# Weight halves stored in 16 KB runs, and three waits moved, in a one-layer transformer and mixture-of-experts step

## What is computed

```python
def expert_choice_moe(h, w_router, w_gate, w_up, w_down):
    cap = CAPACITY_FACTOR * T // N_EXPERTS              # 64 latent, 16 context
    logits = einsum('btd,de->bte', h, w_router)
    aff = softmax(logits, axis=-1)
    g, idx = top_k(swapaxes(aff, 1, 2), cap)            # per expert
    xg = h[idx]                                         # gathered rows
    a = einsum('becd,edf->becf', xg, w_gate)            # 1024 x 1024 each
    u = einsum('becd,edf->becf', xg, w_up)
    y = einsum('becf,efd->becd', silu(a) * u, w_down) * g[..., None]
    return zeros.at[idx].add(y)                         # scatter-add
```

## Time and profile before

| | us |
|---|---|
| three runs | 948.62, 950.81, 950.79 |
| median | 950.79 |
| the profiled execution | 950.83 |
| its span, first to last instruction | 948.8 |
| TensorE busy | 887.2 (94% of the span) |
| VectorE, ScalarE, GpSimd busy | 365.1, 216.3, 102.2 |
| mean DMA rate over the span | 284 GB/s |

### The profile page before, as it was taken

One profiled execution on the slowest core, in us unless ns is written; L12 is line 12 of the kernel. 1 busy time (PEld: TensorE's weight loads), 2 busy tenths in 40 slices (PEclk: granted clock), 3 DMA queues, 4 the chain that ended last, 5 costly groups with the idle time before them and its releaser, 6 DMA issues. The chain is left out here.

```text
span 948.8 us, 19908 instructions
## 1 busy us (share of the span) xinstructions
PE 887.2 (94%) x8641; PEld 441.1 (46%) x8641; DVE 365.1 (38%) x974; ACT 216.3 (23%) x528; POOL 102.2 (11%) x137
## 2 busy tenths in 40 slices
PE   3999998899999999889999999999999999999984
PEld 3544444777656565633443443344344343433431
DVE  4255635887767765812031021111113120220135
ACT  3132223766544653410000000000000000000012
POOL 1021200000000000100011011011101101110225
PEclk9999999999899999999999999999999999999997
DMA  9997532300001115979999999999999999999984
GB/s 340 346 368 276 221 135 100 118 1 1 2 1 46 45 46 220 400 270 411 398 398 398 409 398 397 410 398 398 397 409 398 396 409 398 398 408 376 354 303 158
DMA packets 77717, 269.31 MB, mean 284 GB/s; under 512 B 6208, under 2 KB 9984, under 8 KB 77632
## 3 DMA queue, kind: packets, MB, share of 16 engines
q1 hardware_dynamic: 72384, 251.42, 67.7%
q0 software_dynamic: 4160, 13.90, 5.1%
q10 hardware_dynamic: 1088, 2.74, 0.7%
HBM read 252.06 MB, written 15.99 MB: 283 GB/s over the span
## 5 line engine op out<-in xcount | busy, mean ns | idle before, releaser
L954 PE MATMUL ps<-ring,reg 128*32 128x512 f32 x1792 | 201.6, 592 | 0.0
L1814 DVE TENSOR_SCALAR mod<-ps,kt 64x512 f32<-64x512 f32 x30 | 22.5, 749 | 260.6 <-PE ps L954 260.4
L954 PEld LDWEIGHTS ps<-ring,reg 128*32 128x32 f32 x1792 | 58.4, 110 | 113.0 <-issue 104.6
L968 PE MATMUL ps<-ring,values_in 128*32 128x256 f32 x1536 | 92.4, 382 | 4.6 <-DMA ring<-in_w_up 2.3
L1325 ACT ACTIVATE reg<-ps 128x256 f32<-128x256 f32 x16 | 6.2, 385 | 361.8 <-PE ps L1008 361.8
L954 PE MATMUL ps<-ring,kt 128*32 128x512 f32 x768 | 86.8, 592 | 0.0
L810 PE MATMUL ps<-ring,reg 128*128 128x512 f32 x160 | 78.1, 615 | 0.0
L968 PEld LDWEIGHTS ps<-ring,values_in 128*32 128x32 f32 x1536 | 49.3, 110 | 54.8 <-issue 14.6
L656 PE MATMUL ps<-ring,reg_qt 128*128 128x512 f32 x160 | 70.6, 594 | 0.0
L968 PE MATMUL ps<-ring,reg 128*32 128x256 f32 x1024 | 62.9, 388 | 5.6 <-DMA ring<-in_w_down 4.6
L1268 ACT ACTIVATE ring<-ps 128x640 f32<-128x640 f32 (+3 forms) x80 | 44.3, 554 | 74.9 <-PE ps L739 72.4
(11 more groups left out here) (238 smaller groups left out, 999.4 us busy)
## 6 DMA issues: line engine op xcount, KB each, us to landing
ring<-in_w_up SPq DMA_DIRECT2D x32, 2048.0 KB, 23.7
ring<-in_w_down SPq DMA_DIRECT2D x32, 2048.0 KB, 26.2
ring<-in_w_gate SPq DMA_DIRECT2D x16, 2048.0 KB
reg_qt<-in_w_gate SPq DMA_DIRECT2D x16, 2048.0 KB
ring<-in_w_ada SPq DMA_DIRECT2D x12, 2048.0 KB, 14.7
reg<-in_x_sample SPq DMA_DIRECT2D x8, 512.0 KB, 6.2
ring<-in_w_in SPq DMA_DIRECT2D x2, 2048.0 KB, 17.1
ring<-in_w_out SPq DMA_DIRECT2D x2, 2048.0 KB, 10.1
```

What stands on the lines that cost most here:

```text
L954: last = pe.matmul(o[64 * n + r:64 * n + r + 32, :], x(4 * hf + j, r), w[:, j, n * HALF:(n + 1) * HALF], start=(hf == 0 and j == 0), stop= ...
L968: last = pe.matmul(o[32 * q:32 * q + 32, :], x(c), w[:, j, q * QUART:(q + 1) * QUART], start=(c == 0), stop=(c == KC - 1))
L1814: dve.tensor_scalar(put_l[:, n * HALF:(n + 1) * HALF], ps[rows, 3, :], g_l[rows, e:e + 1], None, ALU.mult)
```

## The change

It has two parts.

The first moves waits. Expert 0's gate halves (slots 0 and 1) now wait for the last scores, and only slot 2 and what follows wait for the last product with the values. The wait for the first latent gather ahead of expert 1's gate is gone. On TensorE `turn_lists` goes ahead of `turn_rows_c(1)`, and the filler matmuls between them are dropped. On ScalarE the copy of the turned context activations goes ahead of the second `modulate_c`.

The second gives partition p the rows `4 p + j` (j from 0 to 3) of each half, which lie together in DRAM: a 16 KB run for each partition where there were four of 4 KB. The contraction then needs its other operand in the same order. So every transpose that feeds it takes every fourth column (`feature_block`, and `j:HALF:4` for the latent activations); the modulation's columns are made in four transposes where there were two, with more small copies; the router weights and the pre-FFN gains are loaded in that order, by nine more DMAs. For the context activations the order is made earlier: in the gate and up products `product_c` reads its moving operand with a step of four elements (16 bytes), in two runs of 128 (`by_block`). The down products and all of `product_l` read their weights as before, element by element in a row.

```diff
+        def feature_block(row, c):
+            return row.rearrange("p (h q j) -> p h j q", h=2, j=4)[:, c // 4, c % 4, :]
...
-        N_CONSTS = 10
+        N_CONSTS = 19
...
+                wr_rows = A["w_router"][0].rearrange("(h p j) e -> h p j e", h=2, j=4)
+                sp.dma_start(wr[:, 0:4 * E].rearrange("p (c e) -> p c e", e=E),
+                             wr_rows[0]).then_inc(consts_in, 16)
+                sp.dma_start(wr[:, 4 * E:].rearrange("p (c e) -> p c e", e=E), wr_rows[1]).then_inc(consts_in, 16)
+                ffn_columns = A["g_pre_columns"].rearrange("(q j) (m h b) -> b h m q j", j=4, m=2, h=2)
+                for b, h in itertools.product(range(4), range(2)):
+                    sp.dma_start(gpre[32 * b:32 * b + 32, KC + 4 * h:KC + 4 * h + 4], ffn_columns[b][h][1],
+                                 allow_slow_non_contiguous=True).then_inc(consts_in, 16)
...
             def expert_weight(e, kind, half, s):
                 w = (A["w_gate"], A["w_up"], A["w_down"])[kind]
-                src = w[0].rearrange("e (c p) n -> e p c n", p=P)[e][:, 4 * half:4 * half + 4, :]
-                sp.dma_start(ring_slot(s).rearrange("p (c n) -> p c n", c=4), src).then_inc(slot_in[s], 16)
+                src = w[0].rearrange("e (h p j) n -> e h p (j n)", h=2, j=4)[e][half]
+                sp.dma_start(ring_slot(s), src).then_inc(slot_in[s], 16)
...
             for s in range(SLOTS):
                 sp.wait_ge(*freed[unit_before(len(UNITS), s)])
                 if s == 0:
+                    sp.wait_ge(scores_done, len(HEAD_UNITS))
+                if s == 2:
                     sp.wait_ge(pv_done, len(HEAD_UNITS) // 2)
                 expert_weight(0, s // 2, s % 2, s)
-            sp.wait_ge(scores_done, len(HEAD_UNITS))
             sp.wait_ge(rows_c_stored, 16)
             sp.wait_ge(rows_stored, 16 * LT)
             sp.wait_ge(x1_turned, 2 * TILES)
-            sp.wait_ge(gathered_l, 16)
...
-                for j in range(2):
-                    last = pe.transpose(ps[:, 7, j * P:(j + 1) * P], modq[:, m, j * P:(j + 1) * P], ident[:, :])
+                for j in range(4):
+                    last = pe.transpose(ps[0:P // 2, 7, j * P:(j + 1) * P], modq[:, m, j:QUART:4], ident[:, :])
...
-                    last = pe.transpose(ps[:, 5 + c // 4, c % 4 * P:(c % 4 + 1) * P], xg_l[:, c * P:(c + 1) * P], ident[:, :])
+                    last = pe.transpose(ps[:, 5 + c // 4, c % 4 * P:(c % 4 + 1) * P], feature_block(xg_l, c), ident[:, :])
...
+                by_block = ring_slot(s).rearrange("p (c h q j) -> p c h j q", c=4, h=2, j=4)
...
                     for q in range(4):
                         last = pe.matmul(o[32 * q:32 * q + 32, :], x(c),
-                                         w[:, j, q * QUART:(q + 1) * QUART], start=(c == 0), stop=(c == KC - 1))
+                                         w[:, j, q * QUART:(q + 1) * QUART] if down else by_block[:, j, q // 2, 2 * (q % 2):2 * (q % 2) + 2, :],
+                                         start=(c == 0), stop=(c == KC - 1))
...
-                    last = pe.transpose(TA[:, j * P:(j + 1) * P], a_l[:, j * P:(j + 1) * P], ident[:, :])
+                    last = pe.transpose(TA[:, j * P:(j + 1) * P], a_l[:, j:HALF:4], ident[:, :])
...
             product_c(3, GC[:, QUART:], context_of(0)).then_inc(up_c, 1)
+            turn_lists()
             turn_rows_c(1)
-            keep_busy(3, 4)
-            turn_lists()
...
             silu_c()
+            copy_turned_c(0)
             modulate_c(1)
-            copy_turned_c(0)
...
             def columns(m):
                 n = COLS[m]
                 dve.wait_ge(modcol_done, n + 3)
                 for cond in (0, 1):
+                    for u in (0, 1):
+                        part = slice(P // 2 * u, P // 2 * (u + 1))
+                        last = dve.tensor_copy(cmod[part, n, cond, :].rearrange("p (h j) -> p h j", h=2), cols[:, u, :, :, cond])
+                if n % 2:
+                    dve.wait_ge(consts_in, 16 * N_CONSTS)
+                    link(last)
+                    for cond in (0, 1):
+                        g = gpre[:, (n // 2) * KC:(n // 2 + 1) * KC]
+                        last = dve.scalar_tensor_tensor(cmod[:, n, cond, :], cmod[:, n, cond, :], 1.0, g, ALU.add, ALU.mult)
                 last.then_inc(modcol_ready, 1)
```

More of the change, by code:

```diff
@@ L823, in turn_x1 @@
                     last = pe.transpose(out_at(o)[:, half, c * P:(c + 1) * P],
-                                        xr[:, t, (4 * half + c) * P:(4 * half + c + 1) * P], ident[:, :])
+                                        feature_block(xr[:, t, :], 4 * half + c), ident[:, :])
                 last.then_inc(x1_turned, 1)
@@ L925, in turn_rows_c @@
                 for c in range(KC):
-                    last = pe.transpose(ps[:, 5 + c // 4, c % 4 * P:(c % 4 + 1) * P], xg_c[:, c * P:(c + 1) * P], ident[:, :])
+                    last = pe.transpose(ps[:, 5 + c // 4, c % 4 * P:(c % 4 + 1) * P], feature_block(xg_c, c), ident[:, :])
                 last.then_inc(xc_turned, 1)
@@ L957, in product_l, with product_c @@
                 return last
-            def product_c(s, o, x, arriving=False):
+            def product_c(s, o, x, down=False, arriving=False):
                 w = ring_slot(s).rearrange("p (c n) -> p c n", c=4)
+                by_block = ring_slot(s).rearrange("p (c h q j) -> p c h j q", c=4, h=2, j=4)
                 hf = s % 2
@@ L1024, in expert @@
                 pe.wait_ge(actT_c_ready, e + 1)
-                product_c(4, YC[:, 0:QUART], acts_c)
+                product_c(4, YC[:, 0:QUART], acts_c, down=True)
                 if final:
                     weight_in(5, e)
-                    product_c(5, YC[:, 0:QUART], acts_c).then_inc(down_c, 1)
+                    product_c(5, YC[:, 0:QUART], acts_c, down=True).then_inc(down_c, 1)
                     pe.wait_ge(actT_l_ready, e + 1)
@@ L1035, in expert @@
                 weight_in(5, e)
-                product_c(5, YC[:, 0:QUART], acts_c)
+                product_c(5, YC[:, 0:QUART], acts_c, down=True)
                 product_l(5, Y, acts_l).then_inc(down_b, 1)
@@ L1096, in _ @@
             act.dma_start(ident[:, :], A["identity"]).then_inc(early_in, 16)
-            act.dma_start(gpre[:, :], A["g_pre_columns"]).then_inc(early_in, 16)
+            act.dma_start(gpre[:, 0:KC], A["g_pre_columns"][:, 0:KC]).then_inc(early_in, 16)
             b_rows = A["b_ada"][0].rearrange("(m q n) -> q m n", m=N_MOD, q=4)
@@ L1427, in modulate_x @@
                                   ALU.mult, ALU.add).then_inc(ht_ready, 1)
-            cols = ps[:, 7, 0:2 * P].rearrange("p (j q r) -> p q j r", j=2, q=4)
+            cols = ps[0:P // 2, 7, :].rearrange("p (j h u r) -> p u h j r", j=4, h=2, u=2)
             def columns(m):
@@ L1434, in columns @@
                 for cond in (0, 1):
-                    dst = cmod[:, n, cond, :].rearrange("p (q j) -> p q j", j=2)
-                    if n % 2 == 0:
-                        last = dve.tensor_copy(dst, cols[:, :, :, cond])
-                    else:
-                        g = gpre[:, (n // 2) * KC:(n // 2 + 1) * KC].rearrange("p (q j) -> p q j", j=2)
-                        last = dve.scalar_tensor_tensor(dst, cols[:, :, :, cond], 1.0, g, ALU.add, ALU.mult)
+                    for u in (0, 1):
[7 more added lines that the diff above has]
+                        last = dve.scalar_tensor_tensor(cmod[:, n, cond, :], cmod[:, n, cond, :], 1.0, g, ALU.add, ALU.mult)
                 last.then_inc(modcol_ready, 1)
```

2 lines of the change are left out of this document (removed).

## The result

| | before | after |
|---|---|---|
| median, four executions each | 950.80 | 1063.24 |
| lowest and highest | 948.62, 951.96 | 1062.36, 1065.37 |
| span of the profiled execution | 948.8 | 1061.1 |
| TensorE busy | 887.2 | 1006.1 |

A forecast was written before the change was run, and what follows sets the result against it. TensorE and the DMA stream were both taken as near their limit among the experts, the stream slightly too slow. 950.8 + 28.2 (gathers) - 8 (weight waits) + 0 (transition) + 2 (tail) + 0.5 (transposes) = 973.5 us; range 941.5 to 1065 us.

The forecast's parts named there:

- the third cost of the second part: Gate and up context products, 64 in all, read their moving operand with a 16-byte step; forecast at no cost.
- the tiles' lost concurrency: Upper bound for the strided context products: four tiles no longer run together, 5 us more a product, 340 us in all.
- The strided rival: Strided read halves the column rate in 64 context products, +112 us; total 1064 us, chance 0.27.
- 8 us of waits gone: TensorE's waits for expert weights vanish, -8 us; in the forecast by a faster stream, in the strided rival by slower TensorE.
- Its 9 us for weight loads with a step: Strided rival's term for loads of the turned operands: half of 141 ns more for 128 of them.
- The 1.7 us of the lists: At the transition to the experts, lists turned at 403.1 us, 1.7 us sooner; forecast nets it to 0, strided rival keeps it.
- The packets: Weight stream on SP's queue: 16 KB runs stay whole as packets of 612 ns, stream at 428 instead of 400 GB/s.
- 12 to 14 forecast: Sign of the forecast: latent gathers land 12 to 14 us after issue; at most 9 in the fast rival.
- the term of 4.7 us a turn: Long packets delay gather and scatter, so TensorE waits 4.7 us more at each of six latent turns, 28.2 us.
- 5.2 (1.7 + 3.5): First part's gains with 4 KB packets: 1.7 us from the lists, 3.5 us from the stream's lead over TensorE.
- 0 or less if the gather meets expert 1's gate halves: Lower bound on the lists' gain; halves expected issued near 393 us, taking 10.5 us, just out of the first gather's way.
- 3.5 of 9.6 us: Earlier gate halves put the stream some 4 us ahead of TensorE, taking about 3.5 us of the 9.6 us of waits.

The follow-up runs named there:

- the run where the delay shows: Kernel before with only the weight halves loaded in 16 KB runs a partition, no strided read and old waits: 991.86 us, ratio 1.045.
- the run with 8 KB: Kernel before with the moved waits, 8 KB runs a partition, turned operands read with a step of two, gathers as late as before: 964.94 us, ratio 1.018.

## Why the prediction was right or wrong

**The direction and the range held, the forecast didn't.** The step that failed is the third cost of the second part: "I take no cost in the forecast, as every matmul row has one rate". All those rows were reads in a row, so they said nothing of a read with a step; a bound was available (the tiles' lost concurrency, 340 us), and I took the end that the rows are nearest to. The runs showed 3.63 us for a product with a step against 1.72 without: 1.91 us each, 122 us in all, where the sum had nothing. ("One rate" was read a little too evenly: the earlier trace rows give 78.1 us / 160 = 0.49 us for 512 columns over the whole array, not 0.45; that changes neither case much.)

**The strided rival had the mechanism.** It took 112 us for the products (122 measured), 8 us of waits gone (TensorE's waits for expert weights, 6.9 us before, are gone), and the gathers hidden behind three slower products, which the 14.1 us from issue to turn show. Its 9 us for weight loads with a step was too much: a load takes 212 ns instead of 141, longer by half, as it assumed, but it runs ahead, and eight transposes take 1.13 us instead of 1.04, four 0.65 instead of 0.60, about 2 us in all. The 1.7 us of the lists were not won. That its total, 1064 as printed and 1062 as its terms add up, lies within 2 us of the measurement is partly luck: the products were put 10 us too low, and the loads 7 us too high. The loads in the profile:

```profile
L943 PEld LDWEIGHTS ps<-ident,reg x64: 196/212/218, 419.6 to 922.5; 128*128 128x128 f32 x64
```

The rule that spoke for it is that full bandwidth needs two hits in each line of 16 bytes (the Trainium skill, SBUF — State Buffer, Specifications). The runs agree for a moving operand: one element in 16 bytes 3.63 us, two 1.80 to 1.85, four 1.72. The same page of the Trainium skill, in its note on SBUF cachelines, calls a step of four fp32 free. For a moving operand the runs show otherwise: three kinds of product were halved.

**The packets were right** in size (16 KB) and time (608 ns against 612), and in the run that has them alone also in the landing of a gather (13.9 us, 12 to 14 forecast). In the changed kernel, whose stream leaves the engines idle at times, it was 10.4 us, and no turn but the first waited for it. In the run where the delay shows, the term of 4.7 us a turn was mis-sized: the waits are 6.0 us, and the clock at half speed behind them adds some 2.3 us a turn that the sum did not have. With 8.3 us instead of 4.7 the forecast would have been 995 us, and the kernels with 16 KB runs and no halved read gave 992 to 1008. The working of the term, 3.6 us for the gather and up to 2.3 us for the scatter ahead of it, isn't borne out either: issued ahead of that scatter, the gathers still took 14.2 us, 6 us more than 8.2.

**The first part** won 4.4 us where the sum had 5.2 (1.7 + 3.5), by other steps. The lists were turned as early as TensorE allowed (403.23 us), but the 1.7 us turned into a loss of 4.7 at the start of the latent products: the bound "0 or less if the gather meets expert 1's gate halves" came true, since these were issued at 395.5 us and not near 393, with stores behind them. The waits for weights fell by 5.9 us, from 6.9 to 1.0, not by 3.5 of 9.6 us. In the changed kernel the lists were turned 10.8 us after they were ready (414.10 against 403.26 us), behind the two slow up products, and its latent products start at 422.48 us instead of 413.01.

**Why the parts don't add up.** The step alone costs 108 us, the 16 KB runs alone 42.5, the moved waits win 4.4, and all together cost 112, not 146. Slower context products between the scatter ahead of a gather and the turn are cover for the gather. Taking the step out therefore won 60 us and not 108, because it took the cover away.

**Small items.** The nine more DMAs, the transposes and copies of the modulation cost nothing that the runs show: the changed kernel turns the last affinities at 391.35 us, the kernel before at 391.12, and runs without these items between 389.67 and 392.82. The first gather of context rows (12.2 and 13.0 us to landing, before 8.3 and 8.6) stood in the sum with no more than the 1.7 us that it was to take back; TensorE waits 4.5 us for it in the changed kernel, and 0.7 before.

**Left open.** Why the gap of 2.43 us in the run with 8 KB was not followed by a lower clock and those of 1.79 and 1.94 us were, the runs don't show; nor how many of the stream's packets one packet of a gather waits for.

## What to carry to other kernels

When a change alters how an operand is read, rows of operands read in a row say nothing of its price: measure one product with the new pattern first, and read at least two fp32 elements of every 16 bytes together. Before the weights' transfers are made longer, look for the small transfer that something waits for and issue it early; moving its issue was worth 49 us here. Price a wait of TensorE with the slower clock behind it, and never add up parts that are each other's cover.

## What the runs showed of the hardware

- A matmul whose moving operand takes one fp32 element out of 16 bytes streams at half the rate: 632 ns instead of 382 (128x256, four tiles), 7.18 us instead of 3.44 for 32 of 128x512, 1086 ns instead of 615 over the whole array. With two of four elements, neighbours or alternate, it is 5 to 8% slower than in a row.
- The stationary operand is another matter: a weight load of 128 columns takes 206 to 210 ns with a step of two elements and 210 to 216 with a step of four (medians of groups), against 141 in a row, so there a step of 8 bytes is not free. Loads of 64 columns with a step of four were seen at both levels: 217 ns in the context activations' eight products, 137 ns in the changed kernel's transposes of the modulation. The runs don't show why.
- After waits of 4.8 to 7.3 us at a latent turn TensorE was granted 0.50 on the restart, every time, and 1.00 again 2.8 to 6.1 us later. After waits of up to 1.53 us it was not, and between 1.79 and 2.76 us both were seen.
- A gather of 128 rows of 4 KB beside a full stream landed after 8.2, 10.1 and 13.9 us (medians) for stream packets of 159, about 300 (968 packets in 100.2% of 18 us) and 608 ns.
